# Inverse by levels: two of three transposes X moved from TensorE to VectorE's 32x32 blocks, a unit's norm issued earlier, zeroes written by GpSimd

## The reference

```
S = S * w_t + sa * b_t + v_t * k_t      (sa = S . a_t)
o_t = S . r_t
o = (o - mean(o)) * rsqrt(var(o) + eps) * gn_w + gn_b     per head of 64
```

## Time and profile before

| what | value |
|---|---|
| median of three runs | 3003.76 us (3002.83 to 3004.73) |
| the profiled execution | 3004.44 us, span 3002.6 us |
| PE busy | 2942.5 us, 98% of the span |
| weight loads of PE | 2367.6 us, 79% |
| VectorE busy | 1686.2 us, 56% |
| ScalarE busy | 1247.3 us, 42% |
| GpSimd busy | 279.7 us, 9% |
| the second block's lanes | about 1778 to 2893 us of the span |

### The profile page before, as it was taken

One profiled execution on the slowest core, in us unless ns is written; L12 is line 12 of the kernel. 1 busy time (PEld: TensorE's weight loads), 2 busy tenths in 40 slices (PEclk: granted clock), 3 DMA queues, 4 the chain that ended last, 5 costly groups with the idle time before them and its releaser, 6 DMA issues.

```text
span 3002.6 us, 39945 instructions
## 1 busy us (share of the span) xinstructions
PE 2942.5 (98%) x15626; PEld 2367.6 (79%) x15626; DVE 1686.2 (56%) x3028; ACT 1247.3 (42%) x2193; POOL 279.7 (9%) x513
## 2 busy tenths in 40 slices
PE   8999999999999999999999999999999999999997
PEld 7878878787878887777778877877878787787886
DVE  6555555545453335565653346666666666666557
ACT  5444443434333325454443234343444434344322
POOL 0110100001000000000000002020120202023101
PEclk9999999999999999999999999999999999999999
DMA  4222222222233322222233323132222313126244
GB/s 171 79 85 78 85 78 84 84 79 84 80 124 134 119 97 72 77 72 71 71 109 140 128 92 93 57 95 73 83 87 71 100 57 101 62 88 204 80 153 155
DMA packets 86794, 289.16 MB, mean 96 GB/s; under 512 B 12096, under 2 KB 12864, under 8 KB 86352
## 3 DMA queue, kind: packets, MB, share of 16 engines
q1 hardware_dynamic: 71184, 246.42, 24.2%
q0 software_dynamic: 15424, 40.19, 4.4%
HBM read 261.26 MB, written 25.17 MB: 95 GB/s over the span
## 4 chain that ended last, share of the span: by engine, by line
PE 92%; DVE 4%; ACT 2%; issue 2%; DMA 0%; DVEq 0%; ACTq 0%
PE bank L283 18%; PE bank L285 17%; PE bank L284 17%; PE bank L287 7%; PE bank L289 7%; PE bank L288 7%; PE bank L1383 2%; PE bank L340 1%; PE bank L320 1%; PE bank L1292 1%; PE bank L469 1%; PE bank L482 1%; PE bank L1313 1%; PE bank L1320 1%; ACT mc_split L566 1%
## 5 line engine op out<-in xcount | busy, mean ns | idle before, releaser
L283 PE MATMUL bank<-ma_split,mc_split 128*128 128x512 f32 x2304 | 954.6, 414 | 22.9 <-DVE mb L1807 14.2
L736 DVE TENSOR_TENSOR mc_split<-mc,mc_split 128x1024 fp32r<-128x1024 f32 x434 | 534.8, 1233 | 766.4 <-ACT mc_split L566 765.6
L285 PE MATMUL bank<-ma_split,mc_split 128*128 128x512 f32 x2304 | 904.3, 392 | 0.0
L284 PE MATMUL bank<-ma_split,mc_split 128*128 128x512 f32 x2304 | 902.0, 391 | 0.0
L566 ACT ACTIVATE mc_split<-mc 128x1024 fp32r<-128x1024 f32 x434 | 457.2, 1055 | 583.7 <-PE bank L287 321.3
L283 PEld LDWEIGHTS bank<-ma_split,mc_split 128*128 128x128 f32 x2304 | 435.1, 189 | 132.9 <-issue 58.4
L285 PEld LDWEIGHTS bank<-ma_split,mc_split 128*128 128x128 f32 x2304 | 434.0, 188 | 96.1
L284 PEld LDWEIGHTS bank<-ma_split,mc_split 128*128 128x128 f32 x2304 | 436.1, 189 | 80.0 <-issue 5.5
L287 PE MATMUL bank<-mc_split,ma_split 128*128 128x512 f32 x576 | 232.0, 403 | 4.0 <-DVE mb L1807 2.4
L289 PE MATMUL bank<-mc_split,ma_split 128*128 128x512 f32 x576 | 225.5, 392 | 0.0
L288 PE MATMUL bank<-mc_split,ma_split 128*128 128x512 f32 x576 | 225.1, 391 | 0.0
(11 more groups left out here) (366 smaller groups left out, 3605.4 us busy)
## 6 DMA issues: line engine op xcount, KB each, us to landing
mc<-in_w SPq DMA_DIRECT2D x434, 512.0 KB, 3.6
x<-mc POOLq DMA_DIRECT2D x8, 1024.0 KB, 5.2
y<-mb_split SPq DMA_DIRECT2D x28, 256.0 KB, 2.6
ma_split<-y POOLq DMA_DIRECT2D x28, 256.0 KB, 4.6
mb<-in_xt SPq DMA_DIRECT2D x8, 512.0 KB, 8.9
mc<-in_x POOLq DMA_DIRECT2D x4, 1024.0 KB, 5.5
mc<-x POOLq DMA_DIRECT2D x4, 1024.0 KB, 7.7
mats<-mc POOLq DMA_DIRECT2D x32, 128.0 KB, 2.2
```

Source lines behind the costliest of these rows:

```text
L283: mm = pe.matmul(banks[j][:], wh[:, c], act_hi[:, kt, :], start=(kt == kts[0]), stop=False)
L284: pe.matmul(banks[j][:], wl[:, c], act_hi[:, kt, :], start=False, stop=False)
L285: last = pe.matmul(banks[j][:], wh[:, c], act_lo[:, kt, :], start=False, stop=(kt == kts[-1]))
L736: dve.tensor_tensor(w_low[:, s % NR, :, :], w_raw[:, s % NR, :, :], w_high[:, s % NH, :, :].bitcast(F32), ALU.subtract).then_inc(w_lo, 1)
```

## The change

- X of levels 4 and 5 is done by VectorE: one transpose instruction per half, 128x512 from `xt` to `xw`, which transposes every 32x32 block in its place. PE and ScalarE have no X step there any more. VectorE, not PE, waits for `xt_in`, and PE's W waits for VectorE. Level 6 stays as it was.
- The points of the level steps become 100, 103, 106, 106, 110, 112, 117, 119, 121 (before: 100, 102, 105, 107, 110, 112, 115, 117, 120).
- The END steps of units 0 to 6 go to points 164, 167, 175, 180, 183, 186 (before: 178, 181, 184, 187, 190, 193). SP's store of the unit follows, one slot earlier.
- The eighth hg head gets the spacing of the others up to step 8 and four points per step after it.
- GpSimd clears `m8` as soon as the first block's last row statistics are there, instead of VectorE in unit 0.

```diff
                 if i < 13:
-                    return begin + 100 + 5 * (i - 4) // 2
+                    return begin + (100, 103, 106, 106, 110, 112, 117, 119, 121)[i - 4]
...
-                return begin + 178 + 3 * (i - CHUNK_K)
+                return begin + (164, 167, 175, 180, 183, 186)[i - CHUNK_K]
 
             def hg_at(h, m):
 
-                return 128 * h + 65 + m * (40 if h == UNITS - 1 else 45) // 10
+                if h == UNITS - 1 and m > 8:
+                    return 128 * h + 101 + 4 * (m - 8)
+                return 128 * h + 65 + 9 * m // 2
...
-                for what, eng in (("X", "act"), ("W", "act"), ("T", "dve")):
-                    CHUNK += [(f"{what}{lv}{p}", 4 + p, eng) for p in range(2)]
+                blocks32 = lv < LEVELS - 1
+                for what, eng in (("X", "dve" if blocks32 else "act"), ("W", "act"), ("T", "dve")):
+                    CHUNK += [(f"{what}{lv}{p}", 0 if what == "X" and blocks32 else 4 + p, eng) for p in range(2)]
...
-                    for p in range(2):
+                    for p in range(2) if part or lv == LEVELS - 1 else ():
                         mats = range(4 * p, 4 * p + 4)
                         if part == 0:
-                            if lv == FIRST_LEVEL:
-                                pe.wait_ge(xt_in, 16 * (u + 1))
-                                c_wait(pe, "dve", u, f"G{2 * NCH - 1}")
-                            else:
-                                c_wait(pe, "dve", u, f"T{lv - 1}{p}")
+                            c_wait(pe, "dve", u, f"T{lv - 1}{p}")
...
-                            c_wait(pe, "act", u, f"X{lv}{p}")
+                            c_wait(pe, "act" if lv == LEVELS - 1 else "dve", u, f"X{lv}{p}")
...
-                if 4 <= i < 13 and (i - 4) % 3 < 2:
+                if 4 <= i < 13 and (i - 4) % 3 < 2 and i not in (4, 7):
...
                         bounds_dve(dve, st, 0)
-                        dve.memset(m8, 0.0).then_inc(m8_zeroed, 1)
                         st(dve.memset(att, 0.0))
...
                     lv = FIRST_LEVEL + (i - 4) // 3
+                    for p in range(2) if i % 3 == 1 and lv < LEVELS - 1 else ():
+
+                        if lv == FIRST_LEVEL:
+                            dve.wait_ge(xt_in, 16 * (u + 1))
+                        else:
+                            c_wait(dve, "dve", u, f"T{lv - 1}{p}")
+                        to, frm = [x[:, 4 * p:4 * p + 4, :].rearrange("p q n -> p (q n)") for x in (xw, xt)]
+                        dve.transpose(to, frm).then_inc(c_dve, 1)
...
             def second_pool(pool):
+                pool.wait_ge(rb_ready, 3)
+                pool.memset(m8, 0.0).then_inc(m8_zeroed, 1)
                 pool.wait_ge(m8_zeroed, 1)
```

## The result

The kernel after takes **2954.14 us** (median, 2953.76 to 2957.04), against 3004.24 of the kernel before in the same runs: a ratio of 0.9834, 95% interval 0.9817 to 0.9851. The profiled execution took 2953.92 us, with a span of 2952.1; that of before had 3002.6, so 50.5 us of span went. The forecast was 2956.

A forecast was written before the change was run, and what follows sets the result against it. PE, busy 98% of the span, bounds the kernel. X 14.1, norm 23.0, eighth head 6.1 and zeroes 5.2 sum to 48.4 us, so 3004.4 becomes 2956 us; range 2950 to 2960, with rival 1 and part of rival 2 to 2972.

The forecast's parts named there:

- X, 14.1 us: Levels 4 and 5: 16 groups of PE transposes at 0.88 us each leave PE's program, 14.1 us less.
- the upper row, 1.22: Price of one VectorE block transpose: the scan's 1.22 us was the nearest row above the 0.69 taken.
- The estimate of 1.24 us: VectorE transpose priced from the skill's 311 ns, four times; the sum would be about 3 us worse.
- X4's margin: X4 on VectorE, awaiting xt's DMA, is ready before W4 on PE: no wait, 0.3 to 0.9 us in hand.
- The norm, 23.0 us: END steps moved ahead in the hg block: all seven L1807 waits, their aftermath and L1241's wait go, 23.0 us.
- Rival 2: At hg block ends another step holds VectorE, L1807 stays late and the 23.0 us stay: 2979 us, chance 0.08.
- The eighth head, 6.1 us: Later step points in the eighth head remove the 2.9 us wait for L1828 and 3.2 of half clock: 6.1 us.
- Zeroes, 5.2 us: First unit: m8 cleared on GpSimd removes 1.3 and 2.2 us of waits and 1.7 of half clock: 5.2 us.
- The 0.6 us that were to stay of L1739's wait: First unit: of PE's 2.8 us wait for L1739, 0.6 us was forecast to remain.
- the bound of 5.3: Clearing m8 on GpSimd: 4096 elements take at most 5.3 us, 16 times the 0.33 us for 256.
- The half clock in these sums: Gains from PE's full clock: 5.0 us behind L1807's waits, 3.2 behind the eighth head's, 1.7 in the first unit.
- Rival 3: VectorE f32 transposes cost several passes, PE stands at W4 and W5; slower from 2.7 us each, chance 0.04.

The follow-up runs named there:

- alone: One part of the change put into the kernel before: X 2988.65 us, the norm 2978.51, the eighth head 2998.11, the zeroes 2997.08.
- The old points: Kernel after with the level steps back at the points of the kernel before: 2960.39 us.
- the double transposes: Kernel after with each of VectorE's 32 block transposes done twice: 2967.44 us, ratio 0.9889 to the kernel before.
- five points: Kernel after with the END steps of units 0 to 6 starting at point 173, five ahead of the kernel before: 2961.31 us.
- Three times: Kernel after with each of VectorE's 32 block transposes done three times: 3032.01 us, ratio 1.01 to the kernel before.

## Why the prediction was right, point by point

**X, 14.1 us: right**, alone 14.2, and 1.77 us in a unit by the distance of equal points in the two traces. The price was taken at 0.69 us and measured 0.687; the upper row, 1.22, didn't hold. The estimate of 1.24 us took the Trainium skill's figure for 128 columns of bf16 ("VectorE: DVE Perf Modes", The three transpose paths) four times; the trace shows 0.687 us for 512 columns of f32, and the measurement decides.

**X4's margin: no wait, as forecast, but for another reason and with less in hand.** I had the pair end 2.5 us after PE passes point 100, held up by the DMA of `xt`, W4 2.8 us after it, and 0.3 to 0.9 us in hand. In unit 1 PE has passed that point's three matmuls near 1986.55. `xt`, issued at 1980.97, lands 4.6 us later, near 1985.5: 1.0 us before PE is there, not 1.2 us after. What X4 stands behind is the split L736, itself 1.74 us late from ScalarE's. Point 100 is the fifth of its slot, and VectorE does a slot's split ahead of the steps of its points 4 to 7; the prediction had the split behind X4, and this step of it was wrong. With `xt` as late as predicted, near 1987.75, X4 would still have begun only behind the split, which ends at 1988.73. The pair ends at 1989.95, 3.4 us after PE passed the point; W4 comes at 1989.60 and its second half at 1990.09. Over the eight units the first half of X4 is ready 0.10 to 0.37 us before W4 needs it, the second 0.05 to 0.26.

That `xt` came some 2.2 us sooner against PE than reckoned has three parts: from the last store of the matrices to the load it took 26.92 us instead of 27.66, the landing 4.6 instead of 5.6, and PE passed the point 32.5 us after that store, not 32.0. Why the load lands sooner stays open. In unit 7 alone, issued 28.84 us after the store and 5.9 us on its way, it lands 2.1 us after PE has passed the point, just as the split ends. The old points and the double transposes agree with a margin that small: one point sooner, or 0.6 us more per half, and W waits in all eight units.

**The norm, 23.0 us: right**, alone 24.3; the blocks give 4.10, 4.02, 3.05, 3.06, 4.05, 3.07, 3.06, together 24.4. The three of about 4 are those behind which the clock had read 0.50. The 1.4 us too few lie in the other four blocks, 0.35 us each: two restarts, one behind the wait for L1807 and one behind L1241's, cost about 0.2 each beside their rows. For the three the 1.67 already held this. Rival 2 gave the take-over 0.7 us in hand. With five points a block restarted 0.84 us after the take-over began (1960.42 to 1961.26); from 1959.45 that is 1960.29, and PE came at 1960.81: 0.5 us in hand.

**The eighth head, 6.1 us: right for the profiled execution.** Between the two traces its stretch gained 6.5 (8.2 from 2776 to 2876 us, less X's 1.77). Alone it timed 4.7, and its trace has 6.3 there.

**Zeroes, 5.2 us: right for the profiled execution**, alone 5.8, 5.9 in the trace. The 0.6 us that were to stay of L1739's wait are gone too. The memset took 3.53 us, below the bound of 5.3.

**The half clock in these sums was in part luck.** 9.9 of the 48.4 us (5.0, 3.2 and 1.7) are stretches at 0.50 that one execution of the kernel before happened to have. Four traces here have the standstills behind L1807: 0.50 follows three, four, two and three of their seven, so the 5.0 us are near what is usual. Four have the eighth head's standstill (2.6 to 2.9 us) and four the first unit's (2.8 us): 0.50 follows each in the trace of the kernel before and in none of the other three. X alone has both, at the full clock (columns as in rows 4):

```profile
2786.60:2793.40 6.80, 6.80 (x60) 5.75 (x60) 5.64 (x11) 2.41 (x5) 0.00 (x0) 1.00 0.03 11
1813.70:1817.10 3.40, 3.40 (x18) 2.87 (x19) 1.68 (x6) 2.16 (x5) 0.00 (x0) 1.00 0.00 0
```

So the 3.2 and 1.7 us are the price in that execution and not in each: the traces of X, the norm and the eighth head alone, which leave the zeroes as they were, run the first unit's stretch 1.6 us faster than that execution did. The eighth head's median of 4.7, between 2.9 and 6.1, fits this; runs of the kernel before, by which it is measured, spread over 8 us, too wide to show it.

**The sum** was 48.4 us and the median gained 50.1. Everything named as a sign of it came, but for those 0.6 us. The forecast subtracts its half-clock terms from the time of the execution that had them (3004.4), so 2956 doesn't hang on how often they come; the gain against a median does.

**Rival 3's price was wrong.** I had it eat the gain at 2.5 us a transpose, by the stall alone. Three times stands in for a transpose of some 1.9 us (1.30 for two, 0.61 more) and is already 1% slower than before; twice, 1.3 us, is 1.1% faster. The break-even lies between, because the stalls bring the half clock in every unit. The trace of before showed that price, and I used it for the gain and not for the loss. It didn't matter at 0.69.

## What to carry to other kernels

When a step is moved ahead, write down the whole chain from its first producer to the instruction that the busy engine waits for, with the split or copy that shares its queue: its length in points of the busy engine's row, less the points it was moved, is the wait that is left. Price a standstill of TensorE at its row, the restart of about 0.2 us and the half clock that may follow, on the side of the loss as on that of the gain. Look for that half clock in the traces of several executions: behind the same standstill it can come in one and not in the next. For a transpose whose data lie in blocks of 32x32 on the diagonal, VectorE's transpose is a bargain where VectorE has 0.7 us to spare.

## What the runs showed of the hardware

- How long one standstill is doesn't tell whether the half clock follows. None followed seven of 1.7 us at block starts; it followed two to four of seven of 2.4 us, in other blocks in other executions, and in one trace of four the 2.9 us of the eighth head and the 2.8 us of the first unit. With three transposes it followed 1.2 and 1.4 us close together, ahead of the small products of W, in every unit, and the single 1.3 us that came 11 to 13 us later in five units of seven.
- VectorE's transpose of 128x512 f32 took what a product of two such tiles takes (687 and 690 ns), twice in a row 1.30 us.
- GpSimd wrote 4096 f32 a partition in 3.53 us, VectorE in 3.47.
